# Output projection by token rows with the norm along the row, first two token tiles one after the other

## The reference

```python
yp = post_ln(yp, 0.5 * swiglu(yp, ffa_gate, ffa_up, ffa_down), ln1_g, ln1_b)
mp = mix_prompt(yp, ...)            # attention branches + short conv, joined by ONE projection:
#   out = concat([nsa (512), conv (512)]) @ w_out          w_out is (1024, 1024)
yp = post_ln(yp, mp, ln2_g, ln2_b)  # layer_norm(ALPHA * yp + mp)
yp = post_ln(yp, 0.5 * swiglu(yp, ffb_gate, ffb_up, ffb_down), ln3_g, ln3_b)
```

## Time and profile before

| | us |
|---|---|
| median of 3 runs (lowest to highest) | 1357.06 (1356.13 to 1359.03) |
| the profiled execution's own time | 1359.71 |
| its span in the profile | 1358.1 |
| mean granted TensorE clock, share of full | 0.971 |
| PE busy | 1264.8 (93%) |
| DVE busy | 864.7 (64%) |
| ACT busy | 508.2 (37%) |

### The profile page before, as it was taken

One profiled execution on the slowest core, in us unless ns is written; L12 is line 12 of the kernel. 1 busy time (PEld: TensorE's weight loads), 2 busy tenths in 40 slices (PEclk: granted clock), 3 DMA queues, 4 the chain that ended last, 5 costly groups with the idle time before them and its releaser, 6 DMA issues.

```text
span 1358.1 us, 30053 instructions
## 1 busy us (share of the span) xinstructions
PE 1264.8 (93%) x11653; PEld 1150.5 (85%) x11653; DVE 864.7 (64%) x1420; ACT 508.2 (37%) x1015; POOL 375.0 (28%) x326
## 2 busy tenths in 40 slices
PE   6999999999999987999989999896699999999996
PEld 6999999999999976989956666695689999999994
DVE  4786378557738865334546666746776666666667
ACT  4322122223222225232225655414654444444434
POOL 0242035104504405000053453101233333333320
PEclk9999999999999988999979999898799999999998
DMA  4787166236626521322185776153133333333201
GB/s 141 211 218 193 49 202 203 79 108 182 202 77 181 164 64 49 66 63 78 49 280 171 249 237 195 36 156 103 32 118 115 123 112 109 109 109 110 94 32 66
DMA packets 193337, 174.28 MB, mean 128 GB/s; under 512 B 22595, under 2 KB 183538, under 8 KB 192820
## 3 DMA queue, kind: packets, MB, share of 16 engines
q1 hardware_dynamic: 187060, 155.64, 38.6%
q0 software_dynamic: 6144, 16.79, 3.7%
HBM read 168.44 MB, written 8.10 MB: 130 GB/s over the span
## 4 chain that ended last, share of the span: by engine, by line
PE 77%; DVE 12%; ACT 4%; issue 3%; DMA 2%; POOL 0%; SPq 0%; DVEq 0%; ACTq 0%; POOLq 0%
PE ps L859 26%; PE ps L1024 16%; PE ps L987 8%; PE ps L915 7%; PE ps L885 4%; DVE dlo L1917 3%; PE ps L1376 2%; DVE glo L1912 1%; DMA draw<-in_ffa_down_dram 1%; PE ps L1412 1%; PE ps L1392 1%; PE ps L1347 1%; DVE x L1987 1%; PE ps L1334 1%; PE ps L1124 1%
## 5 line engine op out<-in xcount | busy, mean ns | idle before, releaser
L859 PE MATMUL ps<-xh,ghi 128*128 128x272 f32 x1168 | 246.6, 293 | 10.4 <-DVE xl L2220 7.8
L859 PE MATMUL ps<-xl,ghi 128*128 128x272 f32 x1168 | 242.8, 289 | 0.0
L859 PE MATMUL ps<-xh,glo 128*128 128x272 f32 x1168 | 242.1, 289 | 0.0
L786 POOL COPY perm<-landing 128x1024 f32<-128x1024 f32 x64 | 137.0, 2156 | 307.0 <-DMA landing<-in_cache_cmp_kv_dram 307.0
L859 PEld LDWEIGHTS ps<-xh,ghi 128*128 128x128 f32 x1168 | 184.2, 190 | 14.5 <-issue 7.1
L1987 DVE SCALAR_TENSOR_TENSOR x<-ps,x 128x544 f32<-128x544 f32 x176 | 126.8, 720 | 101.7 <-PE ps L915 101.2
L859 PEld LDWEIGHTS ps<-xl,ghi 128*128 128x128 f32 x1168 | 184.9, 190 | 0.0
L859 PEld LDWEIGHTS ps<-xh,glo 128*128 128x128 f32 x1168 | 184.4, 190 | 0.0
L1912 DVE TENSOR_TENSOR glo<-graw,ghi 128x1024 fp32r<-128x1024 f32 x73 | 95.6, 1310 | 98.5 <-ACT ghi L1513 96.5
L1519 ACT ACTIVATE dhi<-draw 128x128 fp32r<-128x128 f32 x176 | 53.5, 307 | 228.1 <-PE ps L915 209.7
L469 POOL DMA_DIRECT2D page<-in_cache_sel_kv_dram x128 | 69.8, 546 | 228.8 <-issue 224.5
(11 more groups left out here) (375 smaller groups left out, 2573.7 us busy)
## 6 DMA issues: line engine op xcount, KB each, us to landing
landing<-in_cache_cmp_kv_dram SPq DMA_DIRECT2D x256, 128.0 KB, 2.5
page<-in_cache_sel_kv_dram SPq DMA_DIRECT2D x128, 128.0 KB, 5.0
page<-in_cache_sel_kv_dram POOLq DMA_DIRECT2D x128, 128.0 KB, 5.2
graw<-in_ffa_gate_dram SPq DMA_DIRECT2D x22, 512.0 KB, 4.6
graw<-in_ffa_up_dram SPq DMA_DIRECT2D x22, 512.0 KB, 4.2
draw<-in_ffa_down_dram SPq DMA_DIRECT2D x88, 128.0 KB, 2.8
graw<-in_w_in_dram SPq DMA_DIRECT2D x44, 256.0 KB, 3.3
pair_w<-in_ffb_gate_dram SPq DMA_DIRECT2D x11, 1024.0 KB, 5.4
```

The source lines that it names most:

```text
L786: pool.tensor_copy(perm[:, :, :, at:at + QUAD].rearrange("p x d a -> p a x d"), landing[j % 2][:].rearrange("p a (x d) -> p a x d", d=HD)) ...
L859: last = nc.tensor.matmul(out[:, h, 0:HALF], a[:, k, :], b[:, k, h * HALF:(h + 1) * HALF], start=(k == 0 and a is hi and b is xhi), stop=( ...
```

## The change

The output projection is turned round: tokens become stationary (128 at a time, four tiles) and the weight rows move, 512 columns at a time. The result lies with tokens on the partitions, so the second norm runs along the row, tile by tile, and each normed tile is transposed back for ffb.

- *Layout.* The 32 sample tokens move to the middle of the 544 columns of `xh`, `xl`, `x`: tiles 0 and 1, samples, tiles 2 and 3 (`tile_cols`, `few_cols`). Half `near` holds tiles 0 and 1 and half the samples.
- *Weights.* `w_out` is loaded as eight chunks of 128 full rows (conv chunks first), each split whole. Chunk 2 is waited for with the last sample's values, chunk 6 with the last unit. The stores of the keys and values (`token_stores`, 22 issues) move on SP ahead of these loads.
- *PE.* For each tile 8 fp32 products with the identity put the residual into PSUM (`residual_rows`), then 8 chunks of 6 matmuls add to it (`out_rows`). Tile 0 takes all its chunks, then tile 1 all of its own; the merge of the samples' attention is between them. The samples have fp32 products of their own (`sample_rows`).
- *Norm.* DVE takes mean and variance with `bn_stats`, normalizes in two steps (`row_norm`); PE transposes (`turned_rows`), ACT copies twice (`turned_high`), DVE makes the low part (`turned_low`).
- *First window of ffb.* Plain products (`plain`, 16 of 12 matmuls, in the order `near` first), no seven-block form; the token sums are made during it, for window 1. `rows_back` goes; `yt` is scaled in place (`rows_scaled`).

```diff
# SP, after the last sample loads
+            token_stores()
...
-                sp.wait_ge(w_lo[s], USES["out"][s] + t // 2 - 1 + ONE)
...
+            def out_weights(i):
+                if i < 2:
+                    sp.wait_ge(q["s_pv0"], R + ONE)
+                elif i == 2:
+                    sp.wait_ge(q["s_pv1"], R + ONE)
+                elif i == 6:
+                    sp.wait_ge(q["pv"], UNITS + ONE)
+                for dst, c0 in wo_raw[i]:
...
+            for i in range(KC):
+                out_weights(i)
# POOL
-            sums(0)
-            pool.wait_ge(normed, 2 * KC)
+            pool.wait_ge(q["x2_high"], QT + 1)
+            pool.tensor_tensor(t3[2][:], x[:, lower, far], x[:, upper, far], ALU.subtract).then_inc(q["t3_raw"], 1)
+            for g in range(2, 2 * WINDOWS):
                 sums(g)
# PE
+            def residual_rows(t):
+                if t >= 2:
+                    pe.wait_ge(q["row_ready"], t - 1)
+                b = 2 * (t % 2)
+                for k in range(KC):
+                    nc.tensor.matmul(ps[:, b + k // 4, k % 4 * 128:(k % 4 + 1) * 128], x[:, k, t * 128:(t + 1) * 128],
+                                     ident[:], start=(k % 4 == 0), stop=True, skip_group_check=True)
+            def out_rows(t, i):
+                b, k = 2 * (t % 2), (i + R) % KC
+                pe.wait_ge(q["wo_low"], i + 1)
+                if i == R:
+                    pe.wait_ge(q["at_lo"], t + 1)
+                for a, w in ((xh, wo_hi), (xl, wo_hi), (xh, wo_lo)):
+                    for n in range(2):
+                        done = nc.tensor.matmul(ps[:, b + n, :], a[:, k, tile_cols(t)], w[i][:, n * 512:(n + 1) * 512], ...)
+                if i == KC - 1:
+                    done.then_inc(q["out_done"], 1)
+            def sample_rows():
...
+                for i in range(KC):
+                    for w in (wo_hi, wo_lo):
+                        for c in range(4):
+                            done = nc.tensor.matmul(ps[32 * c:32 * c + 32, 6, 0:256], few_rows,
+                                                    w[i][:, c * 256:(c + 1) * 256].bitcast(F32), ...)
...
+            residual_rows(0)
+            residual_rows(1)
             pe.wait_ge(q["m_ready"], 1)
...
-            early_out(0, range(2), mixed[0:3], R, R - 1)
+            for i in range(R):
+                out_rows(0, i)
             pe.wait_ge(q["cb_scaled"], 1)
...
+            for i in range(R, KC):
+                out_rows(0, i)
+            for i in range(R):
+                out_rows(1, i)
             pe.wait_ge(q["ofin_ready"], 1)
...
-            for t in range(2, KC):
-                product(ps[:, 2 * s:2 * s + 2, :], ghi[s], glo[s], xh, xl, KC).then_inc(w_used[s], 1)
-            norm_products(1)
+            for i in range(R, KC):
+                out_rows(1, i)
+            pe.wait_ge(q["os_ready"], 1)
+            sample_rows()
+            residual_rows(2)
+            for i in range(R):
+                out_rows(2, i)
+            turned_rows(0)
+            folded(0, C_YM, q["row_sum"], 1, mean_ready)
+            for i in range(R, KC):
+                out_rows(2, i)
+            residual_rows(3)
+            turned_rows(1)
+            folded(1, C_YV, sq_ready, SQ, var_ready)
+            for i in range(R):
+                out_rows(3, i)
+            turned_samples()
+            for i in range(R, KC):
+                out_rows(3, i)
+            turned_rows(2)
             ffb_products()
# PE, first window of ffb
-                group(0, 0, first_gate)
-                group(0, 1, first_up)
+                pe.wait_ge(q["x2_low"], 3)
+                quarter((0, 1), 0, 0)
+                quarter((2, 3), 0, 1)
+                turned_rows(3)
+                quarter((4, 5), 0, 6)
+                pe.wait_ge(q["x2_low"], QT + 1)
+                quarter((0, 1), 1, 2)
...
+                quarter((6, 7), 1, 3, (1, 0))
# ACT
-            act.activation(xh[:, 0:R, 0:SEQ], po[:], ACT.Copy).then_inc(q["at_hi"], 1)
+            wo_high(2)
             act.wait_ge(q["exponents_ready"], 1)
             act.activation(chunk_w[:], chunk_w[:], ACT.Exp).then_inc(q["powers_ready"], 1)
+            wo_high(3)
             act.wait_ge(q["o_added"], UNITS)
+            heads_high(0)
+            heads_high(1)
+            wo_high(4)
+            wo_high(5)
             act.wait_ge(q["exponents_ready"], 2)
             act.activation(small[:, C_F:C_F + 8], small[:, C_F:C_F + 8], ACT.Exp).then_inc(q["powers_ready"], 1)
+            heads_high(2)
+            heads_high(3)
+            wo_high(6)
+            wo_high(7)
+            second_norm()
...
+            def turned_high(n, t):
+                act.wait_ge(q["turned"], n + 1)
+                act.activation(x[:, :, tile_cols(t)], src, ACT.Copy)
+                act.activation(xh[:, :, tile_cols(t)], src, ACT.Copy).then_inc(q["x2_high"], 1)
# DVE: neg_rep, then
+            wo_low(2)
             dve.wait_ge(q["maxima_in_psum"], 2)
...
             dve.tensor_tensor(chunk_w[:], neg_all[:], cbf[:, :, OB - 1], ALU.subtract).then_inc(q["exponents_ready"], 1)
+            wo_low(3)
             dve.wait_ge(q["powers_ready"], 1)
...
+            heads_low(0)
+            heads_low(1)
+            wo_low(4)
             dve.wait_ge(q["comb_in_psum"], 1)
...
+            wo_low(5)
             dve.wait_ge(q["powers_ready"], 2)
...
             last.then_inc(q["ofin_ready"], 1)
+            heads_low(2)
+            heads_low(3)
+            wo_low(6)
+            wo_low(7)
             dve.wait_ge(q["ofin_in_psum"], 1)
...
-            norm_values(1)
+            second_norm()
+            def row_norm(n, t):
+                at, b = 16 * t, 2 * (t % 2)
+                dve.wait_ge(q["out_done"], t + 1 if t < 2 else t + 2)
+                for h in range(2):
+                    steps(dve.bn_stats(stat[:, at + 6 * h:at + 6 * h + 6], ps[:, b + h, :]))
+                steps.settle()
+                dve.bn_aggr(stat[:, at + 12:at + 14], stat[:, at:at + 12]).then_inc(since("stat_done", 0)[0], 1)
+                steps(dve.scalar_tensor_tensor(wide(yt[:, t, :]), ps[:, b:b + 2, :], stat[:, at + 12:at + 13],
+                                               wide(ln_g[:]), ALU.subtract, ALU.mult))
+                dve.wait_ge(*since("std_rows", n))
+                steps(dve.reciprocal(stat[:, at + 15:at + 16], stat[:, at + 14:at + 15])); steps.settle()
+                dve.scalar_tensor_tensor(yt[:, t, :], yt[:, t, :], stat[:, at + 15:at + 16], ln_b[:], ALU.mult, ALU.add
+                                         ).then_inc(q["row_ready"], 1)
+            def second_norm():
+                row_norm(1, 0)
+                row_norm(2, 1)
...
+                turned_low(1, 1)
...
+                row_norm(3, 2)
...
+                row_norm(4, 3)
+                turned_low(3, 2)
+                first_lower(6)
+                turned_low(4, 3)
```

More of the change, by code:

```diff
@@ L1454, in _ @@
             values_p(UNITS - 1)
-            def early_out(t, halves, chunks, first, last):
-                for k in chunks:
-                    for a, b in ((wo_hi[t], xh), (wo_hi[t], xl), (wo_lo[t], xh)):
-                        for h in halves:
-                            done = nc.tensor.matmul(ps[:, 2 * t + h, 0:HALF], a[:, k, :], b[:, k, h * HALF:(h + 1) * HALF],
-                                                    start=(k == first and a is wo_hi[t] and b is xh),
-                                                    stop=(k == last and a is wo_lo[t]))
-                return done
@@ new lines, in folded, with turned_rows @@
+            def folded(n, col, ready, count, signal):
+                pe.wait_ge(ready, count)
+                nc.tensor.matmul(ps[:, 7, 256 + n:257 + n], fold4[:], small[:, col:col + 1], start=True, stop=True
+                                 ).then_inc(signal, 1)
+            def turned_rows(t):
+                n = t if t < 2 else t + 1
+                pe.wait_ge(q["row_ready"], n + 1)
+                if n:
+                    pe.wait_ge(q["x2_high"], n)
+                for k in range(KC):
+                    last = nc.tensor.transpose(ps[:, 4 + k // 4, k % 4 * 128:(k % 4 + 1) * 128],
+                                               yt[:, t, k * 128:(k + 1) * 128], ident[:])
+                last.then_inc(q["turned"], 1)
@@ L1467, in _, with turned_samples @@
+            def turned_samples():
+                pe.wait_ge(q["row_ready"], 3)
+                for j in range(2):
+                    last = nc.tensor.transpose(ps[:, 7, j * 128:(j + 1) * 128], ys[:, j * 128:(j + 1) * 128], ident[:])
+                last.then_inc(q["turned"], 1)
             pe.wait_ge(q["s_o"], NB + ONE)
@@ new lines, in turned_samples_high, with rows_scaled @@
+            def turned_samples_high():
+                act.wait_ge(q["turned"], 3)
+                for j in range(2):
+                    act.activation(samples_by_chunk(x, j), turned_chunks(j), ACT.Copy)
```

(25 more changed lines are left out.)

686 lines of the change are left out of this document (361 added, 325 removed).

## The result

| kernel | median of runs, us | lowest to highest | profiled execution: own time, span | mean granted clock |
|---|---|---|---|---|
| before | 1358.05 | 1356.13 to 1363.17 | 1359.71, 1358.1 | 0.971 |
| changed | 1337.63 | 1336.13 to 1339.82 | 1338.71, 1337.1 | 0.983 |

The ratio is 0.9845, with a 95% interval from 0.9813 to 0.9877: 20.4 us faster. 1339.2 was forecast.

What follows compares the result with a forecast made beforehand. PE, busy 93% of the span, was taken as the bound, with waits at the serial second norm and the entry into window 1. Window 1's second group 17.9 us earlier gave 1357.06 - 17.9 = 1339.2 us; range 1330 to 1350.

Steps and rivals of the forecast that it cites:

- Step 1: Up to tile 0's last weight chunk: PE waits 6.3 us in three waits, then loses 1.5 us to a low clock.
- Step 2: The rest of the projection, from tile 0's last two chunks: 54.2 us without a wait, ending at 947.9.
- The price of the cover: Tile 2's norm, held up behind tile 1's low part: 8.1 us paid if tile 3's products did not cover it.
- Step 3: Window 0 of ffb: 3.0 us more matmuls, a 2.1 us wait for tile 3's low part, ending at 975.0.
- Step 4: Entry into window 1: 4.0 us of waits plus a 17.2 us group; second group at 996.2, 17.9 us earlier.
- The queues: On SP, 22 stores move ahead of the weights: nothing gained, at worst the last sample's keys 2 us late.
- (a): The row norm or the entry into window 1 is a new bound: 7.6 us more, 1346.8; chance 0.16.
- (b): Tile 0's waits shorter, clock back at once, DVE beats POOL, entry costs 2.1: 7.1 us less, 1332.1; chance 0.13.
- (c): After tile 0's waits TensorE stays at 1.2 GHz through the stretch up to 947.9: slower, 1392; chance 0.06.
- (d): Tiles not overlapped, each norm ready after PE needs it: four times 4.3 us lost, 1356, no change; chance 0.05.

Runs made afterwards that it cites:

- e7_late: Changed kernel with turned tiles 0 and 1 and the turned samples put behind all products of the projection; 1349.58 us, ratio 0.9932.
- e3_fill: Changed kernel with fourteen added products into an unread bank in the place of tile 0's longest wait; 1333.20 us, ratio 0.9817.
- e1_chunks: Changed kernel with tiles 0 and 1 going chunk by chunk together; 1331.59 us, ratio 0.9822.
- e2_negfirst: Changed kernel with the maxima's transpose ahead of the residual products of tiles 0 and 1 on PE; 1334.48 us, ratio 0.9843.
- e6_bn5: Changed kernel with each tile's pair of statistics instructions run five times instead of once; 1343.84 us, ratio 0.9882.
- e4_poolgate: Changed kernel with POOL's third and fourth chunk sums for window 1's first group held until DVE's four token low parts are done; 1335.93 us, ratio 0.9851.
- e5_bn3: Changed kernel with each tile's pair of statistics instructions run three times instead of once; 1338.88 us, ratio 0.9862.
- e14: The changed kernel itself, unedited, run again beside two edited kernels on the same chip; 1337.89 us, ratio 0.9854.
- e9: Changed kernel with the load of window 1's first pair of weights ahead of the down weights on SP; 1337.91 us, ratio 0.9831.
- e12: Changed kernel with tiles 0 and 1 chunk by chunk together and window 1's first load ahead of the down weights; 1329.73 us, ratio 0.9784.

## Why the prediction was right, and where its terms were off

The forecast was 17.9 us less from mark to mark, and 20.3 were measured; 1339.2 against 1337.6 us. The step that was named as the source, the serial norm turned into tiles beside PE's work, is shown by e7_late for about half of the gain. Term by term:

- **Step 1.** Tile 0's chunk 6 was put 21.5 us after the addition's end, and came 21.0 after it. The three waits were named with their order and were 0.79, 0.56 and 3.59 us, 4.9 in place of 6.3, while the work between them took 16.1 in place of 15.2; the clock behind them cost 1.75 in place of 1.5 (e3_fill gives 2.0). The cause was half right. That tile 1 stands behind tile 0 is shown by e1_chunks; that the residual ahead of the maxima's transpose makes DVE late is true of the maxima only, because the merge product holds DVE next (e2_negfirst).
- **Step 2.** 54.2 us were summed up, and 52.8 passed (892.51 to 945.34). "It holds no wait that I can find": there is none. The mis-sized term is the sample rows, 8.7 us with bounds of 8.3 and 9.1; they took 0.59 + 6.91 = 7.5, below both ends. Four products side by side went at 6.91 / 128 = 0.054 us an instruction, where the earlier trace rows gave 0.067 for the same form in `few`. The statistics, which no row of before showed, took 0.69 us for 512 columns, the end that was taken; the other end, 3.4, would have cost about the 6.5 us of e6_bn5, whose norm is nearly as long. A tile's norm was put at 4.3 us, and takes 936.93 to 941.18.
- **The price of the cover** was named at 8.1 us; e7_late gives 11.5. The sum put the sample rows at 0.6 us, where PE waits 4.3 us for their norm (behind tile 1's copies and low part), and had no low clock behind such waits.
- **Step 3.** The window's parts ended at 971.1 instead of 975.0, of which 1.3 us are this step's own: 25.8 us in place of 27.1. The wait of 2.1 us for tile 3's low part was 0.3. In the earlier trace rows POOL had gone first. Here DVE issued 0.04 us ahead, its low part took 1.23 us, and POOL's difference took 3.59. The Trainium skill (SBUF — State Buffer, Who interferes with whom) has the one that issues first keep the shared access for a whole instruction; the rows of both kernels agree (3.59 us is DVE's 1.2 and the 2.47 of the earlier trace rows), and the 0.2 us that the prediction worked out by it is what was nearly found. The price of the meeting wasn't gone, though: DVE's next token difference took 2.65 us instead of 1.29 behind POOL's.
- **Step 4.** The entry was put at 4.0 + 17.2 = 21.2 us and took 22.0 (971.1 to 993.13): waits of 2.53 and 0.39 us, and 3.4 us at half clock behind them (1.7). The two parts that wait were named, with their sizes the other way round: 0.5 was walked for `A11`, which waited 2.53, and 1.6 for `A12`, which waited 0.39. The 4.0 that was taken lies between two bounds, and that it came near is partly luck: the same kernel's second profile loses 1.7 us more there, to the clock. That POOL is "in the way" was seen in the kernel before only; it is here too, and e4_poolgate shows that sums put later are in the way of other instructions of DVE, which has no free time there.
- **The queues.** No cost of the stores that moved ahead of the weights is seen: the last prompt unit is added 0.7 us earlier than before, which is within the spread of that mark, and between the marks no product waits for a load of weights.

The four differences, -0.5, -1.4, -1.3 and +0.8, make the 2.4 us by which the forecast was too slow.

Of the rivals, (a) needs a norm more than some 2 us longer than it is (e5_bn3, e6_bn5). (b) had three parts: DVE did go ahead of POOL and the first waits were shorter, but neither the clock came back at once nor did the entry cost 2.1. (c) would have had the projection at 1.2 GHz; the stage from 902.7 to 945.3 has 1.00. (d) is built in part by e7_late, and even there 9.7 us are left. Where these come from wasn't tried by itself: PE's waits for the norm are 9.8 us there, where they were 18.8 before, two norms still have cover in that run, by the rows the norm's own chain along rows is shorter (4.3 us a tile), and the entry loses 4.8 us to waits and low clock (22.0 - 17.2), where 6.8 were lost before.

Moving the stores of the tokens back behind the weights wasn't tried: their source has to be out before the buffers that lie over it are loaded.

## What to carry to other kernels

A serial norm behind a large product is worth splitting by tiles when each tile's norm on the other engines is shorter than the next tile's products, and the room is found by making the norm longer until PE waits (here 2.7 us more gave a first wait of 0.5, and 5.3 more gave 5.0). When PE must wait for weights, let two tiles share each chunk as it comes: work for PE in the place of its waits gave 6.8 us, moving one link ahead of a chain that passes PE twice gave 0.5. To send the second link (here the small merge product) out early as well wasn't tried. Where two engines exclude each other and one of them has no free time, delaying the other only chooses which instruction pays.

## What the runs showed of the hardware

- After nearly the same wait PE's clock did not behave the same way twice. Ahead of window 1's first part PE waited 2.53 us in the changed kernel and in e1, 2.52 in e14, 2.57 in e3, 1.87 in e9 and 1.90 in e12. The 36 products behind that part then took 5.42, 7.18, 7.09, 4.79, 7.18 and 4.79 us; full speed is 36 x 0.126 = 4.5. The length of the wait doesn't order these.
- At that place the clock didn't fall with the wait, but later: the wait ended at 973.63 and the first six products ran at full speed, before they slowed down to 0.225 us each from 974.5 to 977.9, at a granted clock of 0.51 (1.2 GHz):

```profile
973.63 0.36 PE L1070 MATMUL ps<-xh,slot_hi 128*128 128x272 f32 x1 [2.53 <-DVE slot_lo L2227]
...
974.48 0.43 PE L1070 MATMUL ps<-xh,slot_hi 128*128 128x272 f32 x1
...
976.43 0.59 PE L1070 MATMUL ps<-xh,slot_hi 128*128 128x272 f32 x1 [0.39 <-DVE slot_lo L2227]
```

- Statistics over 512 columns out of PSUM took 0.69 us, as long as a plain DVE instruction of that size there.
- 256-column fp32 products of 32 rows, four side by side, took 0.054 us an instruction in a row of 128, against 0.067 in a row of 16.
